# Two PSUM banks in turn: the expert and query products of a PEER feed-forward layer issued in pairs

## The chip, the cores and the metric

The kernel runs on one core of one Trainium2 chip. The metric is the device time of one execution, in microseconds (us). A core has TensorE (PE in the profile, its weight loads are PEld), VectorE (DVE), ScalarE (ACT), GpSimd (POOL) and SyncE (SP), whose queue issues most of the transfers. PSUM, where TensorE writes its results, has eight banks of 128 x 512 float32.

## The reference

Two transformer blocks for one sequence of 512 tokens of width 1024. The first block ends in a PEER feed-forward layer, and the change lies there. Each token picks 16 of 16384 experts per head, for 8 heads, by product keys; an expert is a row of `u` and a row of `v`.

```python
def block(t):                                  # t: 128 tokens of width 1024
    q = (t @ wq).reshape(PEER_BLOCK, PEER_HEADS, 2, PEER_DQ // 2)
    s = jnp.einsum('tpcd,pckd->tpck', q, sub_keys).astype(jnp.float32)
    s1, i1 = lax.top_k(s[:, :, 0], PEER_TOPK)
    s2, i2 = lax.top_k(s[:, :, 1], PEER_TOPK)
    ...
    idx = jnp.take_along_axis(cidx, pos, axis=-1)
    g = jax.nn.softmax(top, axis=-1)
    a = jax.nn.gelu(jnp.einsum('tpkd,td->tpk', u[idx], t).astype(jnp.float32), approximate=False)
    return jnp.einsum('tpk,tpkd->td', (g * a).astype(t.dtype), v[idx])
```

## The kernel before

`phase_project` and `phase_mix` compute the first block's attention and recurrent mixer, `phase_peer` the output projection and the PEER layer, `second_block` the second block. All lines that the diff touches are in `phase_peer`.

**Dense experts.** For 384 of the 512 tokens (`DENSE`) the layer is computed densely: the products of all 16384 experts with all these tokens ("up"), gelu, multiplication by a gate matrix that is zero where an expert was not picked, and the product with `v` ("down"). The remaining 128 tokens go by gathers: GpSimd fetches picked rows of `u` and `v` with indirect transfers, and VectorE makes the dot products (`dot`, L1580) and weighted sums (`row`, L1656).

**Three products for one.** Every float32 product is made from high and low parts: `split3` issues high x high (L1054), high weights x low moving (L1055) and low weights x high moving (L1056), all into the same PSUM tile, each with its own weight load. A row of the profile names the moving tile first: `ps<-h_low,u_high`.

**The group loop.** Groups of two 128-row weight tiles are worked off in order on TensorE (`for g in range(OUT_G, GROUPS)`): groups 0 to 3 are the output projection (a loop of its own, above), 4 to 11 the query projection `wq` with all 512 tokens, and 12 to 75 the 64 groups of `u` with 384 tokens. Tile x of the loop uses PSUM bank x mod 4; `bank_free(x)` waits until tile x-4 has been evacuated. A tile is 8 slices (`KT`) of the model width, 3 products each: 24 matmuls. `u_mm` counts finished tiles.

For each group ScalarE (in program order) evacuates tile after tile: a copy to `peer_q` in the query projection (L1442), a gelu (L1447) in the up products. Then it makes the high part of the weights of group g+2 (`high`, L1375), which waits for both tiles of group g. VectorE, or GpSimd before group 44, makes the low part (L1585, L1244). TensorE waits for it (`u_split`) at the group's start. SyncE loads the raw weights and spills the gelus to memory.

**Scores and selection.** In groups 6, 8, 10, 12 and at some later ones up to 38 TensorE computes key scores (`scores`, L1275) from the queries, and VectorE selects the top 16. Most of VectorE's time in groups 12 to 43 is this.

**Spreading the gates.** In groups 44 to 67 two batches m of 8 tokens per group are turned into the dense gate matrix. VectorE builds one-hots for a batch (`batch`, L1604 twice and L1607 three times, waiting for the spreading of batch m-2), TensorE multiplies them (`spread`, L1287: 24 small matmuls into two of the banks 4 to 7, waiting for `built` and for the copies of batch m-2), ScalarE copies the two banks to SBUF (L1434, twice). SyncE writes a block of four batches to memory, and ScalarE waits for the write of block n-2 before the first copy of block n. In each group the order on TensorE is: spreading, tile, spreading, tile; on ScalarE: two gate copies, gelu, two gate copies, gelu, high part of group g+2. On VectorE: low part of group g, dots, two batches.

**The down products.** `down(g)` runs for 64 groups. For each of the 8 output tiles n (bank n) it adds the products of the group's two expert tiles j: 6 matmuls of 384 columns, then the next bank. It waits once for the split parts (`v_split`, `w_split`) and in group 0 for the banks 0 to 3 to be evacuated. ScalarE's high part of `v` for group 0 stands before the last-but-one gelu, that of the weighted gates (`high_w(0)`, L1385) before the last.

Of the kernel before, what the change touches and what calls it, by code (L numbers as in the profile page):

```python
# [21 lines left out]
P = 128  # L22
D = 1024
T = 512
C = 256
KT = D // P
# [56 lines left out]
OUT_TILES, OUT_PIECES = TILES_BEFORE + KT, PIECES_BEFORE + 4  # L83
# [922 lines left out]
OUT_G, WQ_G = 4, 8  # L1006
U_G = NKEYS // EXPERT_TILES
GROUPS = OUT_G + WQ_G + U_G
GW2 = EXPERT_TILES * P
# [3 lines left out]
DENSE = T - P  # L1013
# [37 lines left out]
def split3(pe, out, weights, moving, start, stop):  # L1051

    (wh, wl), (mh, ml) = weights, moving
    pe.matmul(out, wh, mh, start=start, stop=False)  # L1054
    pe.matmul(out, wh, ml, start=False, stop=False)  # L1055
    return pe.matmul(out, wl, mh, start=False, stop=stop)  # L1056


def phase_peer(k):


    nc, ps = k.nc, k.ps
# [3 lines left out]
    GE = EXPERT_TILES  # L1066
    TB = TOKEN_BLOCK
    OUT_T, WQ_T = GE * OUT_G, GE * WQ_G
    with ExitStack() as ctx:
        def sb(name, shape, dt=F32, where=ctx):  # L1070
            return where.enter_context(nc.sbuf_tensor(name, shape, dt))

        h_high, h_low = sb("h_high", [P, KT, T], F32R), sb("h_low", [P, KT, T], F32R)
        u_raw = [k.u_first, sb("u_second", [P, KT * GW2])]
        u_high, u_low = sb("u_high", [P, 2, KT * GW2], F32R), sb("u_low", [P, 2, KT * GW2], F32R)
        gel = sb("gelu", [P, 4, DENSE])
        h_tok, row_sum = sb("h_by_token", [P, D]), sb("row_sum", [P, D])
# [30 lines left out]
        v_high, v_low = sb("v_high", [P, 2, GE, D], F32R), sb("v_low", [P, 2, GE, D], F32R)  # L1108
        w = sb("weighted", [P, 2, GE, DENSE])
        w_high, w_low = sb("w_high", [P, 2, GE, DENSE], F32R), sb("w_low", [P, 2, GE, DENSE], F32R)  # L1110
# [11 lines left out]
        u_in, u_hi, u_split, u_mm, u_ev = k.u_in, k.w_highs, k.w_split, k.sem("u_mm"), k.sem("u_evac")  # L1122
        h_hi, h_split, keys_in = k.h_highs, k.h_lows, k.sem("peer_keys_loaded")
# [7 lines left out]
        weighted, w_hi, w_split, d_mm = k.sem("weighted_ready"), k.sem("w_highs"), k.sem("w_split"), k.sem("d_mm")  # L1131
# [122 lines left out]
        @block.tensor  # L1254
        def _(pe):
            def bank_free(x):
                if 4 <= x < 4 + OUT_T:
                    pe.wait_ge(resid, x - 3)
                elif x >= 4 + OUT_T:
                    pe.wait_ge(u_ev, x - 4 - OUT_T + 1)  # L1260

            def square_sum(t):
                pe.wait_ge(e_sq, SQUARES_BEFORE + t + 1)
                return pe.matmul(ps[:, 7, :], k.ones[:], squares[:, t, :], start=t == 0, stop=t == KT - 1)

            def scores(u):
                c, tt = unit_of(u)
                pe.wait_ge(u_ev, UH * c + UH)
                if u == 0:
                    pe.wait_ge(h_tokens, 1)  # L1270
                if u >= 3:
                    pe.wait_ge(s_ready, u - 2)
                for i in range(UH):
                    h = UH * c + i
                    last = pe.matmul(ps[:, 4 + u % 3, i * P:(i + 1) * P], qp[:, h, tt * P:(tt + 1) * P], keys[:, h, :],  # L1275
                                     start=True, stop=True)
                last.then_inc(s_mm, 1)

            def spread(m):
                pe.wait_ge(built, m + 1)  # L1280
                for x, bank in gate_banks(m):
                    if x >= 4:
                        pe.wait_ge(evac, x - 3)
                    for i in range(4):
                        pair, j = divmod(x % 2 * 4 + i, 2)
                        for part in range(3):
                            last = pe.matmul(ps[:, bank, i * P:(i + 1) * P], ones_of[:, m % 2, 1, pair, :, j],  # L1287
                                             gated[:, m % 2, part, pair, :, j], start=part == 0, stop=part == 2)
                    last.then_inc(mixed, 1)

            for g in range(OUT_G):
                pe.wait_ge(u_split, PIECES_BEFORE + g + 1)
                for j in range(GE):
                    x = GE * g + j
                    bank_free(x)
                    for t in range(KT):
                        if x == 0:
                            pe.wait_ge(h_split, TILES_BEFORE + t + 1)
                        cut = slice(t * GW2 + j * P, t * GW2 + (j + 1) * P)
                        last = split3(pe, ps[:, x % 4, :], (u_high[:, g % 2, cut], u_low[:, g % 2, cut]),  # L1300
                                      (h_high[:, t, :], h_low[:, t, :]), t == 0, t == KT - 1)
                    last.then_inc(u_mm, 1)
                    if x >= 2:
                        square_sum(x - 2)
            square_sum(KT - 2)
            square_sum(KT - 1).then_inc(e_sum, 1)
            for g in range(OUT_G, GROUPS):
                s = g - OUT_G
                if g == OUT_G + 1:
                    for t in range(KT):  # L1310
                        cut = ps[:, 4 + t // 4, t % 4 * P:(t % 4 + 1) * P]
                        pe.matmul(cut, h_high[:, t, DENSE:T].bitcast(F32), k.ident[:], start=True, stop=False)
                        last = pe.matmul(cut, h_low[:, t, DENSE:T].bitcast(F32), k.ident[:], start=False, stop=True)
                    last.then_inc(h_turned, 1)
                if g == OUT_G + 2:
                    pe.wait_ge(keys_in, 16)
                for u in units_at[g]:
                    scores(u)
                if g == TURN_AT:
                    pe.wait_ge(selected, 1)  # L1320
                    for tt in range(SELF):
                        for i in range(3):
                            last = pe.transpose(ps[:, 4 + tt, i * P:(i + 1) * P], sel[:, tt, i, :], k.ident[:])
                        last.then_inc(turned, 1)
                pe.wait_ge(u_split, OUT_PIECES + s + 1)
                for j in range(GE):
                    x = GE * g + j
                    for m in batches_at(g, j):
                        spread(m)
                    bank_free(x)  # L1330
                    for t in range(KT):
                        if x == OUT_T:
                            pe.wait_ge(h_split, OUT_TILES + t + 1)
                        cut = slice(t * GW2 + j * P, t * GW2 + (j + 1) * P)
                        n = T if g < OUT_G + WQ_G else DENSE
                        last = split3(pe, ps[:, x % 4, 0:n], (u_high[:, s % 2, cut], u_low[:, s % 2, cut]),
                                      (h_high[:, t, 0:n], h_low[:, t, 0:n]), t == 0, t == KT - 1)
                    last.then_inc(u_mm, 1)

            def down(g):  # L1340
                pe.wait_ge(v_split, g + 1)
                pe.wait_ge(w_split, g + 1)
                b, final = g % 2, g == U_G - 1
                for n in range(KT):
                    if g == 0 and n < 4:
                        pe.wait_ge(u_ev, WQ_T + GE * U_G - 3 + n)
                    for j in range(GE):
                        cut = slice(n * P, (n + 1) * P)
                        last = split3(pe, ps[:, n, 0:DENSE], (v_high[:, b, j, cut], v_low[:, b, j, cut]),
                                      (w_high[:, b, j, :], w_low[:, b, j, :]), g == 0 and j == 0, final and j == GE - 1)  # L1350
                    if final:
                        pe.matmul(ps[:, n, DENSE:T], row_sum[:, n * P:(n + 1) * P], k.ident[:], start=True,
                                  stop=True).then_inc(d_mm, 1)
                if not final:
                    last.then_inc(v_mm, 1)

            pe.wait_ge(evac, 2 * BATCHES)
            for g in range(U_G):
                if g == U_G - 1:
                    pe.wait_ge(row_used, 2 * PICKS)  # L1360
                down(g)
            for t in range(KT):
                pe.wait_ge(f_squared, 2 * t + 1)
                pe.matmul(ps[:, 0, :], k.ones[:], squares_1[:, t, :], start=t == 0, stop=t == KT - 1)
            pe.wait_ge(f_added, 1)
            pe.matmul(ps[:, 1, :], k.ones[:], squares_2[:, 0, :], start=True, stop=True)
# [1070 lines left out]
```

## Time and profile before

| | |
|---|---|
| Time, median of 3 runs | 2480.97 us (2464.84 to 2481.58) |
| Span of the profiled execution | 2471.8 us |
| TensorE busy | 2295.2 us (93%) |
| VectorE busy | 1774.0 us (72%) |
| ScalarE busy | 922.1 us (37%) |
| GpSimd busy | 623.8 us (25%) |
| Mean granted TensorE clock | 0.971 |

The span goes from the first to the last instruction of the profiled execution; for this kernel that is the only time of that execution, and it lies between the runs timed without a profile. A busy share is an average over stages with different limits. Matmuls overlap in the pipeline, so the pace of TensorE is read from the starts of successive matmuls and not from the duration of one.

### The profile page before, as it was taken

How to read it: one execution, taken by the hardware profiler on the slowest of the kernel's cores; microseconds unless marked ns; L12 is line 12 of the kernel's file. 1: busy time of each engine (PE TensorE's matmuls, PEld its weight loads, DVE VectorE, ACT ScalarE, POOL GpSimd, SP SyncE). 2: the span in 40 equal slices, each digit the busy share in tenths (PEclk: the TensorE clock that was granted, in tenths of full speed). 3: DMA queues.
4: the chain of work that ended last, by engine and by line, in shares of the span. 5: the costliest groups of instructions: out<-in, count | busy, mean ns of one | idle time of the engine just before them, and what ended most of it. 6: DMA issues, size and time to landing. Idle time of an engine off the chain costs nothing. (4 is left out here: it accounts for less than half of the span.)

```text
span 2471.8 us, 32266 instructions
## 1 busy us (share of the span) xinstructions
PE 2295.2 (93%) x12787; PEld 2016.3 (82%) x12787; DVE 1774.0 (72%) x2973; ACT 922.1 (37%) x1206; POOL 623.8 (25%) x352
## 2 busy tenths in 40 slices
PE   7999887978998999999999899999999898999997
PEld 2888676756798999899999899999999575577775
DVE  6555687763589999999986787787776657554543
ACT  4222233333232333455553233323233434566332
POOL 0000132311346777422323333333330000000000
PEclk9999999989999999999999899999999998999999
DMA  6677300011236777788989999999994222012221
GB/s 248 203 239 238 137 16 1 1 69 54 99 115 209 251 246 237 274 316 314 343 322 387 346 356 349 354 356 350 353 355 142 96 84 77 26 52 69 63 91 68
DMA packets 178102, 488.72 MB, mean 198 GB/s; under 512 B 13696, under 2 KB 80384, under 8 KB 166432
## 3 DMA queue, kind: packets, MB, share of 16 engines
q1 hardware_dynamic: 141088, 352.43, 41.7%
q0 software_dynamic: 36864, 134.23, 14.1%
q8 instruction: 101, 1.65, 0.3%
q14 instruction: 49, 0.40, 0.0%
HBM read 432.08 MB, written 52.43 MB: 196 GB/s over the span
## 5 line engine op out<-in xcount | busy, mean ns | idle before, releaser
L1054 PE MATMUL ps<-h_high,u_high 128*128 128x384 f32 (+1 forms) x1216 | 430.2, 354 | 41.7 <-POOL u_low L1244 19.1
L1055 PE MATMUL ps<-h_low,u_high 128*128 128x384 f32 (+1 forms) x1216 | 420.9, 346 | 0.0
L1056 PE MATMUL ps<-h_high,u_low 128*128 128x384 f32 (+1 forms) x1216 | 420.8, 346 | 0.0
L1054 PE MATMUL ps<-w_high,v_high 128*128 128x384 f32 x1024 | 344.7, 337 | 11.0 <-DVE w_low L1624 11.0
L1055 PE MATMUL ps<-w_low,v_high 128*128 128x384 f32 x1024 | 343.7, 336 | 0.0
L1056 PE MATMUL ps<-w_high,v_low 128*128 128x384 f32 x1024 | 343.6, 336 | 0.0
L1054 PEld LDWEIGHTS ps<-h_high,u_high 128*128 128x128 f32 x1216 | 230.7, 190 | 56.6 <-POOL u_low L1244 22.1
L1381 ACT ACTIVATE v_high<-v_raw 128x2048 fp32r<-128x2048 f32 x64 | 122.6, 1916 | 347.2 <-PE ps L1056 347.2
L1054 PE MATMUL ps<-h_high,w_high 128*128 128x512 f32 x560 | 227.9, 407 | 25.7 <-DVE h_low L2261 10.2
L1055 PEld LDWEIGHTS ps<-h_low,u_high 128*128 128x128 f32 x1216 | 231.1, 190 | 8.1 <-issue 1.2
L1056 PEld LDWEIGHTS ps<-h_high,u_low 128*128 128x128 f32 x1216 | 230.7, 190 | 8.0
L1055 PE MATMUL ps<-h_low,w_high 128*128 128x512 f32 x560 | 221.3, 395 | 0.0
L1056 PE MATMUL ps<-h_high,w_low 128*128 128x512 f32 x560 | 221.2, 395 | 0.0
L1612 DVE TENSOR_TENSOR v_low<-v_raw,v_high 128x2048 fp32r<-128x2048 f32 x64 | 146.7, 2292 | 101.5 <-ACT v_high L1381 101.4
L1235 POOL DMA_INDIRECT mixT<-in_peer_v,row_index x102 | 144.3, 1415 | 254.9 <-DVE row_sum L1656 238.5
L1054 PEld LDWEIGHTS ps<-w_high,v_high 128*128 128x128 f32 x1024 | 193.6, 189 | 11.6 <-DVE v_low L1612 8.3
L1235 POOL DMA_INDIRECT mixT<-in_peer_u,row_index x103 | 139.2, 1351 | 247.9 <-DVE row_dot L1580 218.8
L1055 PEld LDWEIGHTS ps<-w_low,v_high 128*128 128x128 f32 x1024 | 193.6, 189 | 0.0
L1056 PEld LDWEIGHTS ps<-w_high,v_low 128*128 128x128 f32 x1024 | 193.5, 189 | 0.0
L1447 ACT ACTIVATE gelu<-ps 128x384 f32<-128x384 f32 x128 | 63.9, 500 | 298.4 <-PE ps L1056 170.8
L2152 DVE TENSOR_TENSOR w_low<-w_raw,w_high 128x1024 fp32r<-128x1024 f32 x69 | 84.6, 1226 | 121.0 <-ACT w_high L2026 120.9
L1054 PEld LDWEIGHTS ps<-h_high,w_high 128*128 128x128 f32 x560 | 107.0, 191 | 59.4 <-issue 17.0
(411 smaller groups left out, 4446.3 us busy)
## 6 DMA issues: line engine op xcount, KB each, us to landing
v_raw<-in_peer_v SPq DMA_DIRECT2D x64, 1024.0 KB
w_raw<-in_w SPq DMA_DIRECT2D x99, 512.0 KB, 3.4
u_first<-in_uT SPq DMA_DIRECT2D x32, 1024.0 KB
u_second<-in_uT SPq DMA_DIRECT2D x32, 1024.0 KB
xT<-in_late_w SPq DMA_DIRECT2D x56, 512.0 KB, 4.4
gelu_up<-gelu SPq DMA_DIRECT2D x128, 192.0 KB
gates<-gates_sb SPq DMA_DIRECT2D x12, 2048.0 KB
weighted<-gelu_up SPq DMA_DIRECT2D x64, 384.0 KB
```

The source lines that it names most:

```text
L1054: pe.matmul(out, wh, mh, start=start, stop=False)
L1055: pe.matmul(out, wh, ml, start=False, stop=False)
L1056: return pe.matmul(out, wl, mh, start=False, stop=stop)
L1235: pool.indirect_dma_start(out=row_of(total), out_offset=None, in_=table, in_offset=bass.IndirectOffsetOnAxis(ap=row_no[:, n:n + 1], axis=0))\
L1381: act.activation(v_high[:, g % 2], v_raw[:, g % 2], ACT.Copy).then_inc(v_hi, 1)
L1447: act.activation(gel[:, x % 4, :], ps[:, x % 4, 0:DENSE], ACT.Gelu).then_inc(u_ev, 1)
L1612: dve.tensor_tensor(v_low[:, g % 2], v_raw[:, g % 2], v_high[:, g % 2].bitcast(F32), ALU.subtract)\
L2152: dve.tensor_tensor(wlo[:, i % SPLITS, :], raw[:, i % RAWS, :], whi[:, i % SPLITS, :].bitcast(F32), ALU.subtract).then_inc(w_low, 1)
```

## The change

A new helper, `split3_pair`, issues the three products of two tiles in turn: high x high of tile one, high x high of tile two, high x low of both, low x high of both. The group loop from group 4 on uses it for the two tiles of a group, in two neighbouring banks, slice by slice. For this both spreading batches and both `bank_free` waits come before the first product of the group, and both tiles are finished by the last two matmuls. The down products of all groups but the last use it for output tiles n and n+1 (banks n and n+1), for j = 0 and then j = 1. The last group of the down products keeps the old order. The wait for the query projection's first hidden state goes slice by slice as before, but six products now follow each wait. Number, size and operands of the matmuls stay as they are; so does the order of additions within each PSUM tile. ScalarE, VectorE, GpSimd and SyncE are not edited.

```diff
+def split3_pair(pe, outs, weights, moving, starts, stop, done=None):
+
+    for i, out in enumerate(outs):
+        pe.matmul(out, weights[i][0], moving[i][0], start=starts[i], stop=False)
+    for i, out in enumerate(outs):
+        pe.matmul(out, weights[i][0], moving[i][1], start=False, stop=False)
+    for i, out in enumerate(outs):
+        last = pe.matmul(out, weights[i][1], moving[i][0], start=False, stop=stop)
+        if done is not None:
+            last.then_inc(done, 1)
+    return last
...
                 for j in range(GE):
-                    x = GE * g + j
                     for m in batches_at(g, j):
                         spread(m)
-                    bank_free(x)
-                    for t in range(KT):
-                        if x == OUT_T:
-                            pe.wait_ge(h_split, OUT_TILES + t + 1)
-                        cut = slice(t * GW2 + j * P, t * GW2 + (j + 1) * P)
-                        n = T if g < OUT_G + WQ_G else DENSE
-                        last = split3(pe, ps[:, x % 4, 0:n], (u_high[:, s % 2, cut], u_low[:, s % 2, cut]),
-                                      (h_high[:, t, 0:n], h_low[:, t, 0:n]), t == 0, t == KT - 1)
-                    last.then_inc(u_mm, 1)
+                    bank_free(GE * g + j)
+                n = T if g < OUT_G + WQ_G else DENSE
+                for t in range(KT):
+                    if g == OUT_G:
+                        pe.wait_ge(h_split, OUT_TILES + t + 1)
+                    cuts = [slice(t * GW2 + j * P, t * GW2 + (j + 1) * P) for j in range(GE)]
+                    split3_pair(pe, [ps[:, (GE * g + j) % 4, 0:n] for j in range(GE)],
+                                [(u_high[:, s % 2, cut], u_low[:, s % 2, cut]) for cut in cuts],
+                                [(h_high[:, t, 0:n], h_low[:, t, 0:n])] * GE, [t == 0] * GE, t == KT - 1,
+                                u_mm if t == KT - 1 else None)
...
-                for n in range(KT):
+                for n in range(0, 0 if final else KT, 2):
                     if g == 0 and n < 4:
-                        pe.wait_ge(u_ev, WQ_T + GE * U_G - 3 + n)
+                        pe.wait_ge(u_ev, WQ_T + GE * U_G - 2 + n)
+                    for j in range(GE):
+                        cuts = [slice((n + i) * P, (n + i + 1) * P) for i in range(2)]
+                        last = split3_pair(pe, [ps[:, n + i, 0:DENSE] for i in range(2)],
+                                           [(v_high[:, b, j, cut], v_low[:, b, j, cut]) for cut in cuts],
+                                           [(w_high[:, b, j, :], w_low[:, b, j, :])] * 2, [g == 0 and j == 0] * 2, False)
+                for n in range(KT if final else 0):
                     for j in range(GE):
                         cut = slice(n * P, (n + 1) * P)
...
```

## Rows read from the trace of the kernel before

**Rows 1.** Head of the page: busy time and share of the span, by engine

```profile
PE 2295.2 (93%) x12787; PEld 2016.3 (82%) x12787; DVE 1774.0 (72%) x2973; ACT 922.1 (37%) x1206; POOL 623.8 (25%) x352
```

**Rows 2.** Stretches: their length, busy time (instructions), granted clock, DMA share, GB/s

```profile
core 0: us, PE busy (x) PEld busy (x) DVE busy (x) ACT busy (x) POOL busy (x), PEclk, DMA share, GB/s
...
703.00:1009.00 306.00, 286.20 (x1649) 282.77 (x1647) 295.25 (x856) 103.18 (x121) 208.92 (x79) 0.98 0.68 225
1009.00:1295.00 286.00, 274.45 (x2306) 264.60 (x2305) 274.57 (x390) 161.54 (x168) 85.62 (x63) 0.99 0.84 315
...
1600.00:1900.00 300.00, 300.00 (x1733) 300.00 (x1732) 232.11 (x179) 95.33 (x72) 93.56 (x66) 1.00 0.92 329
```

**Rows 3.** Timeline of TensorE in the down products (start us, duration us)

```profile
1627.60 0.33 PE L1056 MATMUL ps<-w_high,v_low 128*128 128x384 f32 x1
1627.77 0.33 PE L1054 MATMUL ps<-w_high,v_high 128*128 128x384 f32 x1
1627.94 0.33 PE L1055 MATMUL ps<-w_low,v_high 128*128 128x384 f32 x1
```

**Rows 4.** Timeline of TensorE in group 46: second spreading, second tile

```profile
1043.06 1.55 PE L1287 MATMUL ps<-gated_one_hots,one_hots 128*128 128x128 bf16 x24
1044.42 0.42 PE L1054 MATMUL ps<-h_high,u_high 128*128 128x384 f32 x1
```

**Rows 5.** Timeline of VectorE, its work for group 47

```profile
1040.40 2.28 DVE L1585 TENSOR_TENSOR u_low<-u_second,u_high 128x2048 fp32r<-128x2048 f32 x1
1042.61 1.22 DVE L1580 CUSTOM_DVE_ANT_0 mixT<-mixT,h_by_token 128x1024 f32<-128x1024 f32 x1
...
1044.90 1.29 DVE L1604 TENSOR_TENSOR one_hots<-iota,selT 128x1024 bf16<-128x1024 bf16 x2
...
1048.03 1.28 DVE L1604 TENSOR_TENSOR one_hots<-iota,selT 128x1024 bf16<-128x1024 bf16 x2
```

**Rows 6.** Timeline of ScalarE at the end of group 46

```profile
1048.89 0.49 ACT L1447 ACTIVATE gelu<-ps 128x384 f32<-128x384 f32 x1 [2.84 <-PE ps L1056]
1049.28 1.91 ACT L1375 ACTIVATE u_high<-u_first 128x2048 fp32r<-128x2048 f32 x1
1051.08 2.12 ACT L1434 ACTIVATE gates_sb<-ps 128x512 f32<-128x512 f32 x2
```

**Rows 7.** Waits, whole span: us in total, times, longest us

```profile
ACT gates_sb L1434 <- DMA gates<-gates_sb: 63.6, 10, 8.5
...
PE ps L1054 <- POOL u_low L1244: 19.1, 11, 7.3
```

**Rows 8.** Timeline of GpSimd and TensorE in group 19

```profile
777.38 4.62 POOL L1244 TENSOR_TENSOR u_low<-u_first,u_high 128x2048 fp32r<-128x2048 f32 x1 [1.40 <-ACT u_high L1375]
...
783.13 1.05 PE L1275 MATMUL ps<-peer_keysT,peer_q 128*128 128x128 f32 x8
783.94 0.42 PE L1054 MATMUL ps<-h_high,u_high 128*128 128x384 f32 x1
```

**Rows 9.** Timeline: first and last product of group 4, a query evacuation

```profile
601.44 0.77 PE L1054 MATMUL ps<-h_high,u_high 128*128 128x512 f32 x1 [7.25 <-DVE h_low L1493]
...
616.21 0.39 PE L1056 MATMUL ps<-h_high,u_low 128*128 128x512 f32 x1
...
631.10 0.60 ACT L1442 ACTIVATE peer_q<-ps 128x512 f32<-128x512 f32 x1 [4.84 <-PE ps L1056]
```

**Rows 10.** Timeline from the last up products into the down products

```profile
1360.92 0.49 ACT L1447 ACTIVATE gelu<-ps 128x384 f32<-128x384 f32 x1 [5.11 <-DMA gelu_up<-gelu]
...
1361.31 2.28 DVE L1612 TENSOR_TENSOR v_low<-v_raw,v_high 128x2048 fp32r<-128x2048 f32 x1
...
1364.72 0.66 PE L1054 MATMUL ps<-w_high,v_high 128*128 128x384 f32 x1 [2.93 <-DVE w_low L1624]
1365.18 0.52 PE L1055 MATMUL ps<-w_low,v_high 128*128 128x384 f32 x1
```

**Rows 11.** Stretch after that wait (columns as in rows 2)

```profile
1364.50:1367.90 3.40, 3.18 (x10) 3.21 (x11) 2.99 (x6) 1.11 (x2) 0.88 (x1) 0.50 0.91 294
```

More of the change, by code:

```diff
@@ L1343, in down @@
                 b, final = g % 2, g == U_G - 1
-                for n in range(KT):
+                for n in range(0, 0 if final else KT, 2):
                     if g == 0 and n < 4:
-                        pe.wait_ge(u_ev, WQ_T + GE * U_G - 3 + n)
+                        pe.wait_ge(u_ev, WQ_T + GE * U_G - 2 + n)
[5 more added lines that the diff above has]
+                for n in range(KT if final else 0):
                     for j in range(GE):
                         cut = slice(n * P, (n + 1) * P)
[L1349 to L1353, printed above, removed]
+                        split3(pe, ps[:, n, 0:DENSE], (v_high[:, b, j, cut], v_low[:, b, j, cut]),
+                               (w_high[:, b, j, :], w_low[:, b, j, :]), False, j == GE - 1)
+                    pe.matmul(ps[:, n, DENSE:T], row_sum[:, n * P:(n + 1) * P], k.ident[:], start=True,
+                              stop=True).then_inc(d_mm, 1)
                 if not final:
```

## Prediction

> **What bounds the kernel now.** I read the head of the page, then the table of stretches, then the order of time inside the two stages that the diff touches. TensorE is busy for 93% of the span [rows 1]. The changed stages are the group loop (541 to 1362 us) and the expert down products (1362 to 1927 us); the rest of the span is untouched. In the down products TensorE never waits: 1733 matmuls fill 300.00 us, 173.1 ns each [rows 2]. The group loop has two halves. From 703 to 1009 us VectorE is busy for 295 of 306 us and TensorE for 286. From 1009 to 1295 us, where the gate spreading runs beside the up products, both are busy for some 274.5 of 286 us [rows 2]. In that second half neither engine has slack, so the order in which they hand work to each other matters there.
>
> **What alternating the banks can give.** A matmul of 384 columns starts every 173.3 ns. At 2.4 GHz (granted clock 1.00 there) 384 columns are 160 ns, so 13.3 ns a product are overhead. If waiting for the previous product in the same bank caused it, a product whose predecessor wrote another bank would come sooner. The down loop changes its bank after every six products. In [rows 3] the product at 1627.77 is the first in a new bank: it comes 0.17 us after its predecessor, as do the others. The same rows say that a weight tile loaded twice running (high weights, then high weights again) costs the same as a new one. So I take the gain from alternating as 0, in both stages. Its ceiling is 13.3 ns for each of the products that become paired: 63 groups of 48 down, 64 of 48 up and 8 of 48 for the query projection, 6480 in all, 86 us. Strict alternation itself, with every product in another bank, does not occur in these rows; a penalty is therefore not excluded, but the crossings give no sign of one: 1 ns each would be 6.5 us.
> The Trainium skill ("TensorE: Matmul & The Clock Gate", Back-to-back issue gap) gives a gap of N/2.4 + 2.5 ns for isolated warm matmuls. For 384 columns that would be 162.5 ns; this case's trace has 173.3, and by that page up to 10.8 ns could be regained, 70 us for 6480 products. Nothing in the page ties the gap to the bank.
>
> **What the new order does to the hand-overs.** Two things move in the group loop. The first tile of a group is complete at the group's end, not in its middle, and both gate-spreading batches are issued before any of the group's 48 products, where the second used to stand between the tiles. No instruction is added or removed, so the cost is all in waiting.
>
> *Spread stage, 24 groups (44 to 67).* TensorE needs per group 2 x 1.48 us of spreading (24 small matmuls and the change-over: 1043.06 to 1044.42 and its neighbours) and 8.32 us of products, 11.28 us [rows 4]. VectorE needs 2.21 for a low part, 62/24 = 2.6 dot products of 1.15 = 2.97, and two batches of 3.14 = 6.27: 11.45 us [rows 5]. The stage takes 286.1 us from 1009.0 to 1295.1: 16.9 for the first group, whose first batch is late, and 11.70 for each of the 23 others.
> There is a loop over two groups as well: end of group g, its evacuation, ScalarE's high part for group g+2, VectorE's low part, its dots and two batches for g+2, spreading, end of g+2. Now it is, from [rows 4 to 6]: hand-over 0.2, gelu 0.39, high part 1.9, VectorE 11.45, hand-over 0.2, second spreading 1.48, second tile 4.16 = 19.8 us for two groups, 9.9 each. It hides below the 11.45.
> ScalarE takes its work strictly in program order: gate copies of batch 1, gelu of tile 1, gate copies of batch 2, gelu of tile 2, high part of g+2. After the change the gelu of tile 1 waits to the group's end, and behind it are queued the two gate copies (1.85 us to the next instruction, from the merged pair of 2.1) and the other gelu and the high part. The loop becomes 0.2 + 0.39 + 1.85 + 0.39 + 1.9 + 11.45 + 0.2 + 1.48 + 8.32 = 26.2 us for two groups, **13.1 each**. This is above both engines' own needs and becomes the bound. 23 x (13.1 - 11.7) = 32 us. The first group: two batches and then all 48 products give 3.14 + 0.2 + 1.48 + 8.32 = 13.1 us from the first batch's build to the end, where it was 11.3: 2 us. **Sum 34 us.** VectorE and TensorE would then both idle, in alternation.
> Another wait is added: the second spreading needs banks that ScalarE now empties some 2.4 us after the previous group's end; it comes due 1.5 to 2.2 us after it. That is 0.2 to 0.4 us a group, but it lies inside the loop's longer wait. Alone it would be at most 24 x 0.4 = 10 us.
> ScalarE's longest waits here are for the gate writes, 63.6 us in 10 waits [rows 7]. They come before the first batch's copies of a block, finish before the group's end also in the new order, and stand beside the loop, so I cost them at 0. If the writes took longer, they would add to it.
> The waits that appear are 2 to 4 us per group, in two pieces, and the clock can fall. After 2.93 us of waiting at the head of the down products the next products start 0.32 to 0.46 us apart, not 0.17 [rows 10], and the granted clock reads 0.5, its lower level of 1.2 GHz, for 3.4 us [rows 11]. A fall costs some 1 us; 0 to 24 falls are 0 to 24 us. VectorE's waits are split by the first spreading, so I take 1 us in all and keep 20 for the range.
>
> *Before it, groups 12 to 43.* The high part starts 0.39 us later, since two gelus come after the end of the group. GpSimd's low part ends at 782.00 where the scores are due at 783.13 and the products at 783.94 [rows 8]: 0.39 fits into the 1.1. In groups where TensorE does wait for the low part (19.1 us, 11 waits [rows 7]), GpSimd was late with its gathers and not with the high part. Cost 0, at most 11 x 0.39 = 4 us.
>
> *Query projection, groups 4 to 11.* In group 4 the products wait tile by tile for VectorE's low part of the hidden state: the first product starts at 601.44, after 7.25 us of waiting, and the group ends at 616.44 [rows 9]. With both tiles paced together each arrival feeds six products. Twelve at the lower clock (0.427 us: 512/1.2) and 36 at 0.227 are 13.3 us against 15.0: **1.7 us gained**. After groups 5, 7, 9 and 11 the scores wait for ScalarE's copy of the second tile; now two copies of 0.6 us stand behind the end [rows 9], the first of which starts 0.23 us (one product) sooner than the last did: 0.3 us more, **1.2 us lost** in four places.
>
> *Into the down products.* The last-but-one gelu, which stands ahead of ScalarE's high part of the weighted gates, already starts late, at 1360.92, held by a spill. With the new order it can start at 1361.8. The high part then ends at about 1363.1, before VectorE is done with the low part of v at 1363.6 [rows 10]: cost 0, at most 1 us. Within the down products the order between groups and all waits stay as they are: 0.
>
> **Sum:** 34 + 1 - 1.7 + 1.2 = 34.5, with the unknown costs of 0 to 2 us: **35 us**. The profiled execution has a span of 2471.8 us, between the lowest and the median of the three times shown; set against it this is 2507. The median is 9.2 us higher, and I forecast against the median: 2481 + 35 = **2516 us**.
>
> **Rivals.**
> (a) *The bank was the limit* and the 13.3 ns go. Outside the spread stage 5328 products give 71 us; inside, the loop's 48 products give 0.64 per two groups, 8 us. 2516 - 79 = 2437 us; by the page's smaller share some 2452. For it: the overhead is real and constant. Against it: 504 bank crossings in the down products look like [rows 3]. Chance 0.04.
> (b) *The loop is slacker than I add up*, because the second gate copies or VectorE's dots run elsewhere in it, and only the bank wait of the second spreading is left: 10 us at most, some 2488 us. For it: ScalarE is busy for only 161 of 286 us. Against it: its program order is fixed. It needs the loop to lose 3 us per two groups. Chance 0.10.
> (c) *Loop plus clock.* Each pair of waits brings the lower clock for part of the next products; 0.8 us a group, 20 us, 2536 us. For it: [rows 10, 11]. Against it: the single waits stay below 2.9 us in my sum. Chance 0.14.
> (d) *The change does nothing measurable*, the order of products being of no consequence and the hand-overs covered: 2481 us. Against it: a stage without slack on either engine [rows 2]. Chance 0.04.
> The forecast itself has 0.68. It would flip to faster if alternation saved over 6 ns a product.
>
> **How the numbers follow.** The range runs from 2490 (within 2 us of case b) to 2545 (case c and a small penalty of alternation); it leaves out case a, d and half of b, about 0.15. One per cent, some 25 us, is about what a measurement of this kernel can tell from no change. Faster by more: case a, 0.04. Within: cases b and d with a little of the forecast's lower edge, 0.16. Slower: 0.80.
>
> **What would show it.** In the down products 300 us should hold 1733 matmuls again. The 24 spread groups should take 13.1 us each instead of 11.7, with TensorE waiting for the gated one-hots before both spreadings, and VectorE's low part waiting for ScalarE's high part in every group. ScalarE should show gelu, two gate copies, gelu, high part in one run right after the group's last product. A spacing below 170 ns in the down products would refute the first step; spread groups near 11.7 us would refute the loop.

## The result, and the profile after

The changed kernel takes 2510.27 us (median of 4 runs, 2504.91 to 2515.91) against 2477.45 us of the kernel before on the same chip: the two medians are 33 us apart. The ratio on record, which is not the quotient of these two medians, is 1.0152 with a 95% interval of 1.0131 to 1.0173, or 38 us slower; all ratios below are formed like it, and losses and gains in us that are read from ratios are on its scale. The profiled execution has a span of 2508.4 us, 36.6 more than before. The forecast was 35 us slower. One execution each of `before_dots_last` (2691 us) and `both_mends` (8233 us) below was slow and is in no ratio.

The table of stretches of the changed kernel, two stretches of it (columns: length, busy time and instructions of each engine, granted clock, DMA share, GB/s):

```profile
703.00:1009.00 306.00, 284.85 (x1618) 281.94 (x1617) 294.14 (x850) 98.81 (x116) 203.80 (x76) 0.96 0.66 220
1009.00:1295.00 286.00, 249.54 (x2058) 241.06 (x2057) 248.67 (x353) 137.47 (x152) 81.44 (x60) 0.99 0.79 288
...
1640.00:1940.00 300.00, 300.00 (x1732) 300.00 (x1732) 231.49 (x178) 95.32 (x72) 92.93 (x66) 1.00 0.92 328
```

The last row answers to the last of [rows 2]: in the down products 300 us hold 1732 matmuls, against 1733 before. The middle row shows where the time went. In the same 286 us TensorE and VectorE have each lost about 25 us of work (249.54 and 248.67 us busy, where both had 274.5).

To put numbers on it I took the start of each group's last product from both traces and subtracted. All tables of stages below are made so, in us of the profiled execution:

| stage | before | after | difference | forecast |
|---|---|---|---|---|
| groups 4 to 11 | 110.4 | 110.0 | -0.4 | -0.5 |
| groups 12 to 43 | 307.3 | 311.3 | +4.0 | 0 (0 to 4) |
| group 44 | 16.9 | 18.6 | +1.7 | +2 |
| groups 45 to 67, each | 11.70 | 13.06 | +31.2 in 23 | 13.1, +32 |
| groups 68 to 75 | 66.6 | 67.0 | +0.4 | 0 |
| down products, with the way into them | 549.6 | 548.3 | -1.3 | 0 |

The rest (before group 4 and after the down products, code that is the same) differs by +0.9 us, 3.5 more ahead and 2.6 less behind. Such parts move by some us from one execution to the next: behind the down products the fourteen kernels of this document take 557.6 to 565.8 us.

The loop itself can be read off the timelines of the changed kernel. TensorE at the end of groups 54 and 55 (start us, duration us):

```profile
1164.16 0.51 PE L1066 MATMUL ps<-h_high,u_low 128*128 128x384 f32 x2
1165.89 1.54 PE L1300 MATMUL ps<-gated_one_hots,one_hots 128*128 128x128 bf16 x24 [1.22 <-issue]
1169.03 1.54 PE L1300 MATMUL ps<-gated_one_hots,one_hots 128*128 128x128 bf16 x24 [1.60 <-issue]
1170.37 0.60 PE L1062 MATMUL ps<-h_high,u_high 128*128 128x384 f32 x2
...
1178.43 0.51 PE L1066 MATMUL ps<-h_high,u_low 128*128 128x384 f32 x2
1178.78 3.35 PE L1300 MATMUL ps<-gated_one_hots,one_hots 128*128 128x128 bf16 x48
```

ScalarE in the same time:

```profile
1164.53 0.49 ACT L1465 ACTIVATE gelu<-ps 128x384 f32<-128x384 f32 x1 [2.76 <-PE ps L1066]
1164.92 1.98 ACT L1452 ACTIVATE gates_sb<-ps 128x512 f32<-128x512 f32 x2
1166.66 0.56 ACT L1465 ACTIVATE gelu<-ps 128x384 f32<-128x384 f32 x1
1167.09 1.91 ACT L1393 ACTIVATE u_high<-u_first 128x2048 fp32r<-128x2048 f32 x1
```

VectorE:

```profile
1163.89 1.90 DVE L1625 TENSOR_TENSOR gated_one_hots<-one_hots,selT 128x1024 bf16<-128x1024 bf16 x3
...
1167.03 1.90 DVE L1625 TENSOR_TENSOR gated_one_hots<-one_hots,selT 128x1024 bf16<-128x1024 bf16 x3
1169.04 2.29 DVE L1603 TENSOR_TENSOR u_low<-u_first,u_high 128x2048 fp32r<-128x2048 f32 x1
...
1183.36 2.29 DVE L1603 TENSOR_TENSOR u_low<-u_second,u_high 128x2048 fp32r<-128x2048 f32 x1 [3.48 <-ACT u_high L1393]
```

The group's last pair of products starts at 1164.16. ScalarE's gelu, two gate copies, gelu and high part follow in one run from 1164.53 to 1169.00; before, gelu and high part alone took 2.3 us [rows 6]. VectorE starts its low part at 1169.04. TensorE meanwhile waits twice for one-hots: the first batch is ready at 1165.79, the second at 1168.93, and the spreadings start 0.1 us behind them. The profile calls these waits "issue", but the end of VectorE's row is what they follow. Groups come in unlike neighbours, at first 11.5 and 14.9 us long, for a loop that goes over two groups: 26.4 together, where I had summed 26.2. The waits fall mostly into the long ones: the spreadings at 1178.78 follow the products without any. The row of 1183.36 shows the other half of it, VectorE idle for 3.48 us for ScalarE's high part. The waits view has the sum over the stage of the changed kernel:

```profile
DVE u_low L1603 <- ACT u_high L1393: 37.0, 17, 4.5
```

### The profile page after: what moved, and what is told of

It is laid out like the page before. It is cut to its first block and busy times, and to the rows that moved or that the text cites. A ratio compares the mean times of both kernels' runs of the same rounds, so it can differ in the third digit from the quotient of the medians.

```text
span 2508.4 us, 32268 instructions
## 1 busy us (share of the span) xinstructions
PE 2299.1 (92%) x12787; PEld 2022.4 (81%) x12787; DVE 1764.5 (70%) x2973; ACT 911.8 (36%) x1206; POOL 627.1 (25%) x352
## 5 line engine op out<-in xcount | busy, mean ns | idle before, releaser
L1062 PE MATMUL ps<-h_high,u_high 128*128 128x384 f32 (+1 forms) x1152 | 309.2, 349 | 27.6 <-POOL u_low L1257 20.2
L1064 PE MATMUL ps<-h_low,u_high 128*128 128x384 f32 (+1 forms) x1152 | 304.0, 345 | 0.0
L1066 PE MATMUL ps<-h_high,u_low 128*128 128x384 f32 (+1 forms) x1152 | 303.2, 344 | 0.0
L1062 PE MATMUL ps<-w_high,v_high 128*128 128x384 f32 x1008 | 257.2, 336 | 10.5 <-DVE w_low L1642 10.5
L1066 PE MATMUL ps<-w_high,v_low 128*128 128x384 f32 x1008 | 257.0, 335 | 0.0
L1064 PE MATMUL ps<-w_low,v_high 128*128 128x384 f32 x1008 | 256.9, 335 | 0.0
L1062 PEld LDWEIGHTS ps<-h_high,u_high 128*128 128x128 f32 x1152 | 209.9, 192 | 35.7 <-POOL u_low L1257 22.4
L1064 PEld LDWEIGHTS ps<-h_low,u_high 128*128 128x128 f32 x1152 | 213.0, 191 | 5.3
L1066 PEld LDWEIGHTS ps<-h_high,u_low 128*128 128x128 f32 x1152 | 212.3, 191 | 5.3
L1062 PEld LDWEIGHTS ps<-w_high,v_high 128*128 128x128 f32 x1008 | 183.0, 189 | 11.1 <-DVE v_low L1630 7.6
```

What stands on the lines that cost most here:

```text
L1062: pe.matmul(out, weights[i][0], moving[i][0], start=starts[i], stop=False)
L1064: pe.matmul(out, weights[i][0], moving[i][1], start=False, stop=False)
L1066: last = pe.matmul(out, weights[i][1], moving[i][0], start=False, stop=stop)
```

## The experiments

Each was timed against the kernel before on the same chip. The ratio is to the kernel before; the times of a group are from the trace of one execution.

| kernel | ratio (95%) | groups 45 to 67, each | group 44 | groups 68 to 75 |
|---|---|---|---|---|
| before | 1 | 11.70 | 16.9 | 66.6 |
| after | 1.0152 (1.0131 to 1.0173) | 13.06 | 18.6 | 67.0 |
| down_only | 1.0003 (0.9989 to 1.0017) | 11.71 | 17.5 | 66.6 |
| swap | 1.0003 (0.9990 to 1.0017) | 11.62 | 18.6 | 66.6 |
| old_in_spread | 1.0008 (0.9995 to 1.0021) | 11.66 | 18.5 | 66.9 |
| hoist_only | 1.0047 (1.0027 to 1.0068) | 12.14 | 19.0 | 66.6 |
| late_only | 1.0094 (1.0064 to 1.0125) | 12.46 | 16.9 | 67.0 |
| late_dots_last | 1.0027 (1.0010 to 1.0044) | 12.01 | 11.6 | 73.3 |
| pairs_dots_last | 1.0042 (1.0018 to 1.0066) | 11.89 | 14.0 | 71.4 |
| act_order | 1.0078 (1.0048 to 1.0108) | 12.02 | 18.7 | 66.6 |
| both_mends | 1.0005 (0.9988 to 1.0022) | 11.64 | 13.7 | 69.7 |
| pool_pairs | 1.0432 (1.0395 to 1.0469) | 15.17 | 22.9 | 66.8 |
| before_dots_last | 1.0006 (0.9993 to 1.0019) | 11.86 | 11.6 | 70.0 |
| first_dots_last | 0.9981 (0.9967 to 0.9995) | 11.71 | 11.8 | 66.6 |

### Does alternating the banks give or cost anything?

**down_only**: the kernel before with `split3_pair` and the new `down`, and nothing else of the change.

> The kernel before with the paired order in the down products alone; the group loop is as before. Loop theory: alternating the banks gives nothing, so 300 us of the down products hold 1733 matmuls again (173 ns each), the spread groups keep 11.7 us each, and the time is that of before within 0.3%. Rival 'the bank was the limit': 3024 products lose up to 13.3 ns each, 40 us or 1.6% faster, with a spacing of 160 to 163 ns. Rival 'alternation has a price': the spacing exceeds 174 ns, 3 us for each ns.

Ratio 1.0003. The stretch 1600 to 1900 us of its trace:

```profile
1600.00:1900.00 300.00, 300.00 (x1733) 300.00 (x1732) 233.80 (x180) 95.33 (x72) 94.05 (x66) 1.00 0.93 331
```

The mean distance of the down products is 173.35 ns. Both rivals fall.

**swap**: in `split3` the second and third products change places.

```diff
-    pe.matmul(out, wh, ml, start=False, stop=False)
-    return pe.matmul(out, wl, mh, start=False, stop=stop)
+    pe.matmul(out, wl, mh, start=False, stop=False)
+    return pe.matmul(out, wh, ml, start=False, stop=stop)
```

> The kernel before with the second and third product of each triple exchanged, everywhere: high weights x high, low weights x high, high weights x low. No weight tile is then loaded twice running; the bank stays the same through a tile, as before. (The order of additions differs.) The paired order changed two things at once, the bank from product to product and the repeated weight tile. Theory 'neither matters': 173.3 ns a product, the time of before within 0.3%. Rival 'two effects cancel in the paired order' (the bank change saves x, the lost repetition costs x): here only the second acts, the spacing grows above 175 ns, 6 to 10 us for each ns.

Ratio 1.0003, 173.35 ns again. So neither the bank of the previous product nor a repeated weight tile moves the distance, and the null result of `down_only` is not two effects that cancel.

### Where in the kernel is the loss?

**old_in_spread**: the changed kernel, with the old loop for the groups that spread.

```diff
+                if batches_at(g, 0):
+                    for j in range(GE):
+                        x = GE * g + j
+                        for m in batches_at(g, j):
+                            spread(m)
+                        bank_free(x)
...
+                        last.then_inc(u_mm, 1)
+                    continue
```

> The changed kernel, with the old order (spreading, tile, spreading, tile, each tile counted when it is done) in the 24 groups 44 to 67 that spread gates; all other groups and the down products stay paired. Loop theory: the spread groups go back to 11.7 us each and 32 to 34 us of the 37 lost come back: about 2479 to 2484 us on a chip where before takes 2477. What remains is the small cost of groups 4 to 43. Rival 'pairing costs everywhere' (alternation or the late first tile in all groups): most of the loss stays, above 2500 us.

Ratio 1.0008: with everything but 24 of the 72 group-loop groups paired, the loss is gone within the measurement, and the groups are back at 11.66 us.

### Which of the two movements is it?

**hoist_only**: both spreadings first, then tile one and tile two as before.

```diff
+                for j in range(GE):
+                    for m in batches_at(g, j):
+                        spread(m)
                 for j in range(GE):
                     x = GE * g + j
-                    for m in batches_at(g, j):
-                        spread(m)
                     bank_free(x)
```

> The kernel before with one of the two movements in the spread groups: both spreadings are issued before the group's products, but the two tiles are still made one after the other and each is counted when it is done. Loop theory: ScalarE has made the first gelu and all gate copies by the group's end, so the loop over two groups is the 19.8 us of before plus the 4.16 us of a tile, 24.0, or 12.0 us a group: 23 x 0.3 = 7 us and 2 us for the first group, some 9 us (0.35%) slower than before. Rival 'the hoisted spreading is the whole cost' (built one-hots come too late, whatever ScalarE does): 13 us a group, some 34 us slower.

12.14 us a group where 12.0 was expected, and 12 us in all where 9 was. The hoisted spreading is a third of the loss and not the whole.

**late_only**: the order of products and spreadings as before, but in the spread groups `u_mm` counts tile one with the second-last product of the group.

```diff
...
+    pe.matmul(out, wh, mh, start=False, stop=False)
+    pe.matmul(out, wh, ml, start=False, stop=False).then_inc(done, 1)
+    pe.matmul(out, wl, mh, start=False, stop=True).then_inc(done, 1)
...
```

> The kernel before with the other of the two movements: the order of TensorE's products and spreadings is the old one, but in the 24 spread groups the first tile is counted only with the group's last products, so that ScalarE's first gelu, and the second gate copies behind it, come after the group's end. Loop theory: the loop over two groups is 19.8 + 1.85 + 0.39 = 22.0 us, 11.0 a group, below VectorE's 11.45; the time stays within 0.3% of before. Rival 'late evacuation is the whole cost' (the gate copies queued behind the gelu stop TensorE's next spreading): 13 us a group, some 30 us slower.

A miss: 12.46 us a group and 0.9% slower, where my loop gave no change. Reckoning again, I found that the loop has two ways round. I had followed the one by VectorE's second batch. By the first batch it has one batch less on VectorE (3.14) but both spreadings and both tiles on TensorE (11.28 instead of 5.64): 22.3 us for two groups before, 11.15 each, just under the engines' own needs, and 24.5, or 12.3 each, with the late gelu and its gate copies in it. In the changed kernel both spreadings come first, and the way by the second batch, 26.2, is the longer one; so the omission did not touch the forecast. It did need a test, because another cause was open: the late gate copies could hold up TensorE's banks.

**late_dots_last**: `late_only`, with VectorE's dots moved behind its batches in the spread groups, which takes 2.97 us out of both ways round.

```diff
-                for n in dots_at[g]:
+                for n in dots_at[g] if not batches_at(g, 0) else []:
                     dot(n)
...
                 for j in range(GE):
                     for m in batches_at(g, j):
                         batch(m)
+                for n in dots_at[g] if batches_at(g, 0) else []:
+                    dot(n)
```

> late_only (old order on TensorE, first tile counted with the last products) with VectorE's dots behind its two batches instead of ahead of them, in groups 44 to 67. late_only took 12.46 us a group where my loop, reckoned by way of the second batch, gave 11.0. Revised theory: the loop has two ways round, and I left out the one by the first batch: hand-over 0.2, gelu 0.39, gate copies 1.85, gelu 0.39, high part 1.9, low part 2.21, dots 2.97, one batch 3.14, hand-over 0.2, and then the whole 11.28 us of TensorE's group: 24.5 for two groups, 12.3 each. Without the dots in it this is 21.6, 10.8 a group, and VectorE's own 11.45 bounds: 11.5 to 11.8 us a group, within 0.3% of before. Rival 'ScalarE's late gate copies hold up TensorE's banks': the dots don't matter, and it stays at 12.3 to 12.5 us a group, some 0.9% slower than before.

16 of the 23 groups take exactly TensorE's 11.28 us, which the rival excludes. But the mean is 12.01 and not 11.5 to 11.8: four groups take 14.3 to 15.4 us. In each of these four ScalarE's copies have just waited 7.5 to 8.4 us for a gate write, and TensorE waits 1.8 to 2.8 us behind them; ScalarE's waits for gate writes are 62.9 us in 10, where they were 63.6 in 10 before. In the tail (73.3 instead of 66.6 us) one group takes 15.0 us, behind a gelu that waited 9.3 us for a spill. Half of the forecast failed: the loop is opened, and waits on transfers take part of it back.

**pairs_dots_last**: the changed kernel with the same edit on VectorE.

> The changed kernel with the same move: VectorE's dots behind its two batches in groups 44 to 67. Loop theory: the way by the second batch falls from 26.2 to 23.2 us for two groups, 11.6 a group, that by the first batch to 21.6; 11.6 to 11.8 us a group instead of 13.06, so 29 to 33 of the 37 us come back: about 0.3% slower than before. Rival 'TensorE's wait for ScalarE's gate copies (2.4 us after the group's end) is what costs': nothing on VectorE helps, and it stays at 1.5% slower.

Eighteen of the 23 groups take 11.6 to 11.9 us, where the sum said 11.6. The mean is 11.89, with three groups of 13 us, and the ratio 1.0042: 27 of the 38 us (29 to 33 were expected) come back by an edit on VectorE alone, so TensorE's wait for ScalarE's copies was not the cost.

**act_order**: the changed kernel with another order on ScalarE in the spread groups.

```diff
                 for j in range(GE):
-                    x = GE * g + j
                     for m in batches_at(g, j):
...
+                if batches_at(g, 0):
+                    high(g + 2 - OUT_G)
+                for j in range(GE):
+                    x = GE * g + j
...
-                if g + 2 < GROUPS:
+                if g + 2 < GROUPS and not batches_at(g, 0):
```

> The changed kernel with another order on ScalarE in groups 44 to 67: all four gate copies as soon as the spreading is done, then the high part of group g+2, then both gelus. Loop theory: gelu, copies and gelu (2.6 us) leave the loop: 26.2 - 2.6 = 23.6 for two groups, 11.8 a group, so some 28 us come back: about 0.3% slower than before (2480 us). The bank wait of the second spreading goes as well. Rival 'the hoisted spreading alone is the cost': with both spreadings ahead of all products nothing on ScalarE helps, and it stays above 12.5 us a group.

Groups of 11.15 and 12.9 us in turn, 12.02 on average (11.8 expected). By the ratios 18 us are back, by the groups' times 24; some 28 were expected. The part behind the down products, which no edit touches, takes 565.6 us in this trace and 558.1 in that of the changed kernel, so the two figures need not agree. The direction is right and the size short by 0.2 us a group.

**both_mends**: the two edits together.

> The changed kernel with both mends in groups 44 to 67: ScalarE's four gate copies first, then the high part, then both gelus; and VectorE's dots behind its batches. Each alone left 11.9 to 12.0 us a group. Loop theory: the way by the second batch is 0.2 + 1.9 + 2.21 + 6.27 + 0.2 + 1.48 + 8.32 = 20.6 us for two groups, 10.3 each, below TensorE's 11.28 and VectorE's 11.45. 11.3 to 11.6 us in the ordinary group, 11.4 to 11.9 with the waits for gate writes; between before and 0.3% slower in all. Rival 'what is left over 11.3 in the mended kernels is not the loop but transfers (gate writes, gelu spills)': the ordinary group is at 11.28 here, but the average is again 11.9 or more.

This is the changed kernel at the speed of the kernel before: 1.0005. Eleven groups take 11.15 us, 0.13 less than the 11.28 of the old order; they have one change from products to spreading and back, where the old order has two. ScalarE's timeline there:

```profile
1055.43 1.92 ACT L1393 ACTIVATE u_high<-u_second 128x2048 fp32r<-128x2048 f32 x1 [4.53 <-PE ps L1066]
1057.26 0.85 ACT L1468 ACTIVATE gelu<-ps 128x384 f32<-128x384 f32 x2
1065.44 3.90 ACT L1451 ACTIVATE gates_sb<-ps 128x512 f32<-128x512 f32 x4 [7.34 <-DMA gates<-gates_sb]
1069.13 1.92 ACT L1393 ACTIVATE u_high<-u_first 128x2048 fp32r<-128x2048 f32 x1
```

The last two rows show what lifts its mean to 11.64: the four copies wait for a gate write and end only after the group's last product, and the high part comes late. The rival of this run, transfers, is right about the remainder in that sense, though not about its size (11.9 or more).

### A mend that made it worse

**pool_pairs**: the changed kernel with the low part on GpSimd up to group 67 (`if x + OUT_G < POOL_TO`, 68 instead of 44; the same bound on VectorE).

> The changed kernel with the low part of the weights on GpSimd also in groups 44 to 67 (4.6 us there, 2.3 on VectorE), where GpSimd is busy for a third of the time. Loop theory: the batches no longer stand behind ScalarE's high part, so the loop is open. Left are TensorE's 11.28, VectorE's 9.2, and the low part by way of GpSimd: 0.2 + 0.39 + 1.85 + 0.39 + 1.9 + 4.6 = 9.3 us after a group's end, in time for the next but one. 11.3 to 11.6 us a group: about the time of before or up to 0.3% faster. Rival: the two engines disturb one another, or GpSimd is late with the low part because its gathers wait for VectorE's dots, as in groups 12 to 43; then 12 us a group or more.

15.17 us a group, a miss in the rival's direction. Eleven of the 23 groups do take 11.5 to 11.6 us, as the sum said; six take 19 to 28. VectorE's rows, by line, in the spread groups:

```profile
L1626 DVE TENSOR_TENSOR gated_one_hots<-one_hots,selT 128x1024 bf16<-128x1024 bf16 x144 | 125.7, 927 | 1.7
L1599 DVE CUSTOM_DVE_ANT_0 mixT<-mixT,h_by_token 128x1024 f32<-128x1024 f32 x49 | 81.3, 1675 | 60.7 <-DMA mixT<-in_peer_u,row_index 60.7
L1623 DVE TENSOR_TENSOR one_hots<-iota,selT 128x1024 bf16<-128x1024 bf16 x96 | 79.4, 867 | 0.0
```

Both things happen. The dots wait 60.7 us for gathers that GpSimd issues behind its low parts. And three instructions are slower on average: 927, 1675 and 867 ns instead of 687, 1220 and 685 in the changed kernel. The timeline has one of them:

```profile
1188.61 5.11 DVE L1626 TENSOR_TENSOR gated_one_hots<-one_hots,selT 128x1024 bf16<-128x1024 bf16 x1
```

GpSimd's row of the same timeline:

```profile
1188.43 4.73 POOL L1258 TENSOR_TENSOR u_low<-u_second,u_high 128x2048 fp32r<-128x2048 f32 x1 [16.47 <-ACT u_high L1394]
```

VectorE's multiplication, 0.69 us otherwise, starts while GpSimd's subtraction runs, and ends 0.56 us after it. The Trainium skill ("SBUF — State Buffer", Who interferes with whom) says that a VectorE instruction with two inputs in SBUF contends with a GpSimd instruction that reads SBUF, and that the ports they share are an exclusive lock. The trace agrees: 5.11 us for 0.69. It is no single case: beside 21 of the 23 subtractions of groups 44 to 67 one VectorE instruction is stretched in this way, to an end 0.5 to 1.1 us behind the subtraction, and together they take 79 us longer than without; the waits for gathers are 60.7 us. How the 3.6 us a group over the expected 11.6 divide between the two was not measured.

### A version that beats both

**before_dots_last**: the kernel before with VectorE's dots behind its batches in groups 44 to 67.

> The kernel before with VectorE's dots behind its two batches in groups 44 to 67. What the runs so far point to: the way round by the first batch, 22.3 us for two groups before, falls to 19.3 and no longer comes near the engines' own needs; TensorE's 11.28 and VectorE's 11.45 are left. The first group is 5 us shorter, as in late_dots_last (11.6 instead of 16.9). Groups 45 to 67 at 11.3 to 11.6 us, but some longer by 3 where ScalarE waits for a gate write, and 0 to 7 us lost in groups 68 to 75. In all 0 to 0.5% faster than before. Rival: the occasional long groups are the price of the move, and it comes out as in late_dots_last, 0.3% slower.

No difference, 1.0006. Group 44 gains 5.3 us (16.9 to 11.6), and most groups run at 11.28, but five take 12.5 to 15.7 us and the tail takes 70.0 us. The rival is right in kind: the long groups take the gain back. In the two longest (15.7 and 15.2 us) ScalarE's copies have waited 11.0 and 9.8 us for a gate write; ScalarE's waits of this kind are 82.0 us in 10, against 63.6 before. Why the writes are waited for longer stays open.

**first_dots_last**: the same move in group 44 alone.

```diff
-                for n in dots_at[g]:
+                for n in dots_at[g] if g != SPREAD_AT else []:
                     dot(n)
...
+                for n in dots_at[g] if g == SPREAD_AT else []:
+                    dot(n)
```

> The kernel before with VectorE's dots behind its batches in group 44 alone. The other groups keep their order, since moving the dots there cost as much as it gave (11.86 us a group against 11.70, and 3.4 us more in groups 68 to 75). Theory: one dot of 1.15 us and the wait of 2.1 us for its gather leave the way to the first spreading, and the first group takes 11.6 to 13.7 us instead of 16.9; 3 to 5 us (0.1 to 0.2%) faster than before. Rival: the following groups start with VectorE further behind and take it back; no difference.

Ratio 0.9981 (0.9967 to 0.9995): 0.2% faster than the kernel before, the only kernel here that is. Group 44 takes 11.8 us. The next two take 13.0 and 11.9 instead of 11.3 and 11.5; from group 47 on it goes as before. Groups 44 to 67 take 281.0 us in the trace, where they took 286.0.

## Why the prediction was right, step by step

**Alternation gives 0**: right, and the step with the most at stake. `after`, `down_only` and `swap` all show 173.35 ns. The bank crossings of the old order [rows 3] had told it. The 13.3 ns over the 160 of the columns are still there in all three kernels, and nothing here shows what they are; this change regains none of them. The Trainium skill ("TensorE: Matmul & The Clock Gate", Back-to-back issue gap) would have 162.5 ns for isolated matmuls; the measurement decides for 173.35 with these products.

**The loop at 13.1 us a group**: right. 13.06 was measured, and the ScalarE run of gelu, copies, gelu, high part is in the trace as summed. Two of my signs were too wide: VectorE's low part waits for the high part in 17 of the 23 groups and not in every one, and TensorE waits before 28 of the 46 spreadings and not before all, since the loop is worked off in long and short groups. That the loop is the cause is shown from three sides: restoring the old order in its groups alone removes the loss (`old_in_spread`); shortening it on VectorE (`pairs_dots_last`) or on ScalarE (`act_order`) gives back 27 and 18 us by the ratios; both together give back all (`both_mends`).

**The sum of the loop before, 9.9 us a group**: wrong as "the" loop. It was the way by the second batch; the one by the first batch is 11.15. I had written that the loop hides below the 11.45 of VectorE; it hides by 0.3 us and not by 1.5. For the changed kernel this made no difference, for `late_only` it did. In the end neither movement alone is harmless: 0.5% for the hoist, 0.9% for the late tile, 1.5% for both.

**First group +2**: measured +1.7, but that the two agree is luck. `swap` and `old_in_spread` have the old order in group 44 and take 18.6 and 18.5 us there, as much as the changed kernel; `before` and `down_only` take 16.9 and 17.5. The granted clock of group 44 is 0.82 in the first three and 0.90 in the last two. So what the new order costs in this group is not shown.

**Group 4 -1.7, score waits +1.2**: measured -1.2 (25.05 to 23.83 us) and 4 x 0.28 = +1.1 (12.75 to 13.03 us for a group with scores ahead of it).

**Groups 12 to 43 at 0, at most 4**: measured +4.0, at the end of what I had allowed. It is not a constant of the change: `pairs_dots_last`, `act_order` and `pool_pairs` have it too (311.3, 311.2 and 311.4), while `old_in_spread` and `both_mends`, whose order on TensorE is the same up to group 43, take 308.5 and 308.4, and the kernels with the old order 307.1 to 307.4. In the changed kernel the granted clock of this stretch is 0.96 where it was 0.98 [rows 2], TensorE's waits for GpSimd's low part are 20.2 us in 8 instead of 19.1 in 11 [rows 7]; in `old_in_spread` and `both_mends` they are 19.9 in 11. Fewer and longer waits with more time at the lower clock fit the 4 us; why they fall so in four of the six kernels stays open.

**The clock in the spread stage, 1 us, at most 20**: the granted clock from 1009 to 1295 us is 0.99, as before, although TensorE waits: the 28 waits above 0.3 us in groups 45 to 67 are all below 1.9 us, and the clock there is 1.00. It falls in group 44 alone, where TensorE waits 3.64 us and then 0.85: from 1021.0 to 1025.0 us it is 0.50. It falls there in the kernel before too. Rival (c) did not come about; its 2536 us would be a ratio of 1.022. Rivals (a), (b) and (d) are excluded by the interval as well.

**The total**: the forecast of 35 us came out for the reason given, since groups 45 to 67 make up 31.2 of the 36.6 us in the traces, where I had put 32. That the rest agrees too is partly luck: the 4.0 us of groups 12 to 43, which I had put at 0, stand in for the 1 us of the clock, for up to 2 us of unknown costs, and for what the first group may not have cost.

## What to carry to other kernels

Before regrouping work on a busy engine, follow every path from the end of one round back to itself through the in-order queues of the others, each way round and not only the nearest; compare it with the busiest engine's need. Here a reordering that adds no instruction lengthened such a loop from 22 to 26 us per two rounds, because it reported the first half of the work later and asked for the second half of the input sooner. And what a new order of matmuls can gain may be legible in the old trace, as it was here, at the places where the old order happens to do the same.

## What the runs showed of the hardware

- The distance between successive float32r products of 384 columns is 173.35 ns at the full clock whether the bank alternates at each product, at every sixth or never within 24, and whether a weight tile is loaded twice running or not.
- A bf16 multiplication of 128 x 1024 on VectorE, 0.69 us, took 5.11 us beside a 4.73 us subtraction on GpSimd; 21 of 23 such subtractions stretched one VectorE instruction.
- In groups 45 to 67 of the changed kernel 28 waits of TensorE of 0.3 to 1.8 us, 36.9 us in 300, left the granted clock at 1.00. Waits of 3.64 and 0.85 us in group 44 went with 4.0 us at the lower level, and one wait of 2.93 us in the kernel before was followed by 3.4 us at it [rows 10, 11].
